# Turning keys and values of heads 1 to 3 in 32x32 blocks on VectorE with transfers, in place of TensorE transposes

## The chip, the cores and the metric

The kernel runs on one core of one Trainium2 chip. The time is the device time of one execution in microseconds (us), as the median of several runs; one execution was also profiled, and all rows below are from that one. PE is TensorE, DVE is VectorE, ACT is ScalarE, POOL is GpSimd, and SP is the engine that issues nearly all transfers (DMAs).

## The reference

The kernel computes one inference step of a decoder layer for a prompt (512 tokens and 16 meta tokens) and 8 samples of 8 tokens, 592 tokens together, in float32. The part that matters here is branch B, a matrix memory with 4 heads of width 256:

```python
z  = xn @ w_in + b_in          # columns split into ... q | k | v | o ...
s  = einsum('bhtd,bhsd->bhts', q, k) * w
num = einsum('bhts,bhsv->bhtv', s, v) + e_int[..., None] * einsum('bhtd,bhdv->bhtv', q, C)
C_new = decay[..., None, None] * C + einsum('bhs,bhsd,bhsv->bhdv', wk, k, v)
```

The projections come out of TensorE with features on the partitions and tokens along the row. The scores need k in that form. The products with `s` and `wk` contract over tokens, so they need k and v the other way round, with tokens on the partitions. That turned form is what the change makes in another way.

## The kernel before

The 592 tokens are padded to 640 = 5 chunks of 128 (`TT` = 5, `TW` = 640). A head is worked off in one turn of the loop `for h in range(HEADS)`, which every engine has in its own program. In the turn of head `h` TensorE does two things in alternation: the attention work of head `h` (`score(c)`, `values(c)` for chunks c = 0 to 4) and the eight projection tiles of head `h + 1`, `fill(h + 1, n)` for n = 0 to 7. Tiles 0 and 1 are the keys, 2 and 3 the values, 4 and 5 the queries, 6 and 7 the output gate (`PARTS`). Each tile is 48 matmuls (split float32) on one 128-column slice of the weights. Tiles 5 to 7 are cut in twelve pieces, `mix(0)` to `mix(11)`, that lie between the steps of `values(4)` (the chunk with the samples). The piece behind `mix(2)` is the product of the queries with the eight sample states; TensorE waits there for all eight state loads, `c_in[0]` to `c_in[7]`.

For heads 1 to 3, keys and values are turned inside the turn of the head before. `k_tokens(h + 1)` runs after tile 2, `v_tokens(h + 1)` after tile 4, and `last_tokens(h + 1)` (the fifth chunk of both) inside `values(4)`: 8 + 8 + 4 TensorE transposes of 128x128 into PSUM (`ring`), which ScalarE copies to `k_tok` (`kt`) and `v_tok` (`vt`). For head 0 the same happens before the loop.

Weights come through two `stage` slots. SP issues the load of a tile's weights when POOL has finished with the slot (`w_lo`); ScalarE then makes the high part `whi` (L924), POOL the low part `wlo` (L866), and TensorE waits for `w_lo`. SP works strictly in the order of its program, so a wait in it holds back everything behind. Its turn of the loop is:

```python
for n in range(2 if h else 3, 8):
    ...
    head_load(8 * (h + 1) + n)     # weights of tile n of head h + 1
c_load(h, 6)                       # states 6 and 7 of this head, into v_feat
c_load(h, 7)                       # both wait until last_tokens(h + 1) is done
next_load(h, 0)
```

States 6 and 7 are loaded into `v_feat` (`vf`), the buffer from which the values are turned; that is why they wait for the turning.

Of the kernel before, what the change touches and what calls it, by code (L numbers as in the profile page):

```python
# [31 lines left out]
P = 128  # L32
# [72 lines left out]
for h_ in range(-1, HEADS):  # L105

    names = [("proj", h_ + 1, n_) for n_ in range(8)]
    if h_ < 0:

        names[7:7] = [("ltok", 0)]  # L110
        names[6:6] = [("ktok", 0)]
    elif h_ + 1 < HEADS:
        names[5:5] = [("vtok", h_ + 1), ("ltok", h_ + 1)]
        names[3:3] = [("ktok", h_ + 1)]
    for name_ in names:
        TILES[name_] = T_NEXT
        T_NEXT += 1
    if h_ < 0:

        T_WA = T_NEXT  # L120
        T_NEXT += 8
# [138 lines left out]
def hybrid_layer(nc, a, o):  # L260
    w_in, b_in = a["w_in"][0], a["b_in"][0]
    ctx = ExitStack()
    with ctx:
# [151 lines left out]
        ones = sb("ones", [P, P], r + 512)  # L415
        wt = [sb("w_t0", [P, TW], r + 1024), wt1]
        gq = sb("gate_rows", [P, TW], r + 1024 + 4 * TW)
        r += 1024 + 8 * TW
        nst = sb("n_state", [P, NS, 8], r)
        misc = sb("misc", [P, 256], r + 288)  # L420
# [56 lines left out]

            return (m0, HALF), (HALF, T)

        def turned(name, h):  # L480

            if h:
                return wide[TILES[name, h] % 2]
            return bank2(1 if name == "ltok" else 0)

        def ffn_out(n):
# [39 lines left out]
        sq_done, var_done, root_done, nt_scaled, ht_done, head_done = (  # L526
            sem("sq_done"), sem("var_done"), sem("root_done"), sem("nt_scaled"), sem("ht_done"), sem("head_done"))
        x_free = sem("x_free")
        n_turned, n_ready = sem("n_turned"), sem("n_ready")
        guard_ready = sem("guard_ready")  # L530
        qz_zero, pad_zero = sem("qz_zero"), sem("pad_zero")
# [16 lines left out]

        def aview(ap):
            return ap.rearrange("(r c) -> r c", c=P)  # L550

        block = ctx.enter_context(nc.Block())

# [2 lines left out]
        def _(sp):  # L556
# [124 lines left out]
            def c_load(h, idx):  # L681

                if h:
                    sp.wait_ge(c_out[idx], 16 * h)
                if h + 1 == HEADS and idx in (4, 5):

                    sp.wait_ge(head_done, 2 * (HEADS - 1))
                if h + 1 < HEADS and idx >= 6:

                    sp.wait_ge(tile_done, TILES["ltok", h + 1] + 1)  # L690
                sp.dma_start(state(h, idx), a["state_mlstm_C"][0, ORDER[idx], h].rearrange("(i p) v -> p i v", p=P)
                             ).then_inc(c_in[idx], 16)

# [34 lines left out]
            def next_load(h, j):  # L728
# [3 lines left out]
                else:  # L732
                    sp.wait_ge(w_lo, B_WB + j - 1)
                    load(B_WB + j, (B_WB + j) % 2, wb, slice(P * j, P * j + P))

            for h in range(HEADS):
                for n in range(2 if h else 3, 8):
                    if h + 1 == HEADS and n in (5, 6):
                        c_load(h, n - 1)
                    head_load(8 * (h + 1) + n)  # L740

                c_load(h, 6)
                c_load(h, 7)
                next_load(h, 0)
                sp.wait_ge(z_evicted, NZ * h + TT)
                sp.dma_start(o["p_mlstm_C"][0, 0, h].rearrange("(i p) v -> p i v", p=P), cp[h % 2][:, :, 0:DH]
                             ).then_inc(cp_out, 16)
                for idx in range(4):
                    c_store(h, idx)
                next_load(h, 1)  # L750
                if h + 1 < HEADS:
                    for idx in range(4):
                        c_load(h + 1, idx)
                for idx in range(4, 8):
                    c_store(h, idx)
                if h + 2 < HEADS:
                    c_load(h + 1, 4)
                    c_load(h + 1, 5)
                    spread_load(h + 2)
# [156 lines left out]
        def _(act):  # L916
# [242 lines left out]
            def k_tokens(h):  # L1159

                t, s = TILES["ktok", h], h % 2
                evict(t, kt[s][:, 0:4].rearrange("p c d -> p (c d)"), turned("ktok", h)[:, 0:4 * DH], ACT.Copy)

            def v_tokens(h):

                s, z = h % 2, turned("ltok", h)
                dst, src = vt[s][:, 0:4, 0:DH], grouped(turned("vtok", h)[:, 0:4 * DH], DH)
                t = TILES["ltok", h]
                if h:
                    evict(TILES["vtok", h], dst, src, ACT.Copy)  # L1170
                    act.wait_ge(tile_done, t + 1)
                else:

                    act.wait_ge(tile_done, t + 1)
                    st(act.activation(dst, src, ACT.Copy))
                st(act.activation(kt[s][:, 4], z[:, 0:DH], ACT.Copy))
                evict(t, vt[s][:, 4, 0:DH], z[:, DH:2 * DH], ACT.Copy)

# [57 lines left out]
            for h in range(HEADS):  # L1236
                for n in range(8):
                    project_hi(8 * (h + 1) + n)
                    if 1 <= n <= TT:
                        squares(h, n - 1)  # L1240
                    if n == 6:
                        norm_root(h)
                    if n == 7 and h + 1 == HEADS:
                        for f in range(6):
                            act.wait_ge(x_free, f // 2 + 1)
                            hb_split(f)
                    project(8 * (h + 1) + n)
                    if h + 1 < HEADS:
                        if n == 2:
                            k_tokens(h + 1)  # L1250
                            spread(h + 1)
                        elif n == 4:
                            v_tokens(h + 1)


            act.wait_ge(tile_done, T_WB)
# [140 lines left out]
        def _(dve):  # L1397
# [312 lines left out]
            def hb_rest(f):  # L1710

                dve.wait_ge(hb_hi, f + 1)
                tt(xl[:, f, M0:], hb[:, f, M0:], xh[:, f, M0:].bitcast(F32), ALU.subtract).then_inc(hb_lo, 1)

            for h in range(HEADS):
                s = h % 2
                ebc, cpr = ebcs[s], cp[s]
# [26 lines left out]
                for c in range(TT):  # L1744
# [33 lines left out]
                        dve.wait_ge(y_done, n + 1)  # L1778
                        cpy(nt[:, c, :], Y(n)).then_inc(y_evicted, 1)  # L1779

                    if c == 0:
                        dve.wait_ge(tile_evicted, TILES["ltok", h] + 1)
                    if c < 4:
                        keys(c, w[:, P - 1:P])
                        y_evict()
                        update_prompt()
                        if c == 1 and h + 1 < HEADS:
                            mask_add(h + 1)
                        continue
                    keys(c, w[:, TAIL - 1:TAIL])  # L1790
                    for p in range(2):
                        at = PAIR + LS * p + LS - 1
                        st.link(dve.tensor_reduce(wsum[:, p:p + 1], w[:, at:P:2 * PAIR], axis=AX.X, op=ALU.add))
                        keys(TT + p, wsum[:, p:p + 1])
# [28 lines left out]
                    if h + 1 == HEADS:  # L1823
                        hb_rest(0)
                        hb_rest(1)
                    for j in range(2):
                        f = 2 * h + j
                        gcol = cols[:, C_HG + f:C_HG + f + 1]
# [174 lines left out]
        def _(pe):  # L2003
# [206 lines left out]

            def k_tokens(h):

                if h:
                    begin(TILES["ktok", h])
                else:
                    pe.wait_ge(lru_sig, 8)
                    pe.wait_ge(tile_evicted, TILES["proj", 0, 1] + 1)
                tokens(turned("ktok", h), k[h % 2], range(4)).then_inc(tile_done, 1)

            def v_tokens(h):  # L2220

                if h:
                    begin(TILES["vtok", h])
                    tokens(turned("vtok", h), vf, range(4)).then_inc(tile_done, 1)
                else:
                    pe.wait_ge(tile_evicted, TILES["ktok", 0] + 1)
                    tokens(turned("vtok", h), vf, range(4))

            def last_tokens(h):

                if h:
                    begin(TILES["ltok", h])
                pe.wait_ge(pad_zero, min(h + 1, 2))
                tokens(turned("ltok", h), k[h % 2], [4])
                tokens(turned("ltok", h), vf, [4], DH).then_inc(tile_done, 1)

            for n in range(8):
                if 16 + n in LRU_TURN:
# [28 lines left out]
            for h in range(HEADS):  # L2267
# [20 lines left out]
                def values(c):  # L2288

                    n, kap = TT * h + c, NZ * h + c  # L2290
                    pe.wait_ge(p_done, n + 1)
                    if n >= 2:
                        pe.wait_ge(y_evicted, n - 1)
                    last = pe.matmul(Y(n), pt[:, :], vt[s][:, c, :], start=True, stop=c == 0, skip_group_check=True)  # L2294
# [28 lines left out]
                        return  # L2323

                    w = wt[s][:, P * c:TW]
                    for ii in range(2):
                        pe.matmul(NU(n)[:, 16 * ii:16 * ii + 16], kt[s][:, c, P * ii:P * ii + P], w[:, LS - 1:P:LS],
                                         start=False, stop=True, skip_group_check=True)
                    if h + 1 < HEADS:
                        last_tokens(h + 1)  # L2330
                    mix(0)
                    across(P * c, LAST, False)
                    outer()
# [57 lines left out]
                for c in range(TT):  # L2391
                    values(c)
                    if c < 4:
                        score(c + 1)
                        fill(h + 1, c + 1)
                    if h + 1 < HEADS:
                        if c == 1:
                            k_tokens(h + 1)
                        elif c == 3:
                            v_tokens(h + 1)  # L2400

            for f in range(2):
                gemm(B_WB + f, T_WB + f, (B_WB + f) % 2, (T_WB + f) % 2, KT, xh, xl,
# [142 lines left out]
```

## Time and profile before

| | us |
|---|---|
| median of 3 runs (1076.96 to 1077.76) | 1077.06 |
| the profiled execution | 1075.73 |
| its span in the profile | 1073.7 |
| TensorE busy (99% of the span) | 1062.7 |
| VectorE busy (57%) | 608.4 |
| ScalarE busy (37%) | 396.2 |
| GpSimd busy (35%) | 371.6 |
| mean granted TensorE clock | 0.998 |

The three turns that turn keys and values each take 72.9 us or so: the second begins its tile 3 behind 347.35 us, the third behind 420.22 us. Times "at 347.35" are from the start of the span. The profiled execution ran 1.3 us below the median, and 2.0 us of it lie outside the span.

### The profile page before, as it was taken

To read this page: it belongs to the slowest core of one execution; us is meant where nothing else is said; L and a number is where in the kernel's file an instruction comes from. 1 tells how busy PE (TensorE), PEld (TensorE's weight loads), DVE (VectorE), ACT (ScalarE), POOL (GpSimd) and SP (SyncE) were. 2 spreads that over 40 slices of the span, in tenths; PEclk is the share of its full clock that TensorE was granted. 3 is DMA by queue.
4 is the path that set the end of the run, shared out by engine and by line. 5 is a ranking of instruction groups with operands and counts; after the bars stand their busy time and mean duration, and the time that the engine had idled before them with its cause. 6 is when DMAs were issued, how large, how long until landed. Compare 5 with 4: busy or idle time off the path is not lost.

```text
span 1073.7 us, 19483 instructions
## 1 busy us (share of the span) xinstructions
PE 1062.7 (99%) x8034; PEld 1037.8 (97%) x8034; DVE 608.4 (57%) x961; ACT 396.2 (37%) x574; POOL 371.6 (35%) x179
## 2 busy tenths in 40 slices
PE   8999999999999999999999999999999999999997
PEld 7999999999999999999999999999999999999997
DVE  6777458944343242253453338999950189999413
ACT  6566786313332434322432343222311122222332
POOL 4333334332222222222223344333443244334330
PEclk9999999999999999999999999999999999999999
DMA  8433332236254261363442333232323222233312
GB/s 224 136 100 91 103 88 69 79 103 162 59 186 123 71 224 54 89 199 89 140 166 80 91 89 97 81 95 81 101 62 99 74 79 79 79 90 100 99 43 89
DMA packets 180272, 111.80 MB, mean 104 GB/s; under 512 B 7611, under 2 KB 176811, under 8 KB 179934
## 3 DMA queue, kind: packets, MB, share of 16 engines
q1 hardware_dynamic: 179980, 110.55, 35.9%
q8 instruction: 63, 1.03, 0.4%
q14 instruction: 19, 0.16, 0.0%
q10 hardware_dynamic: 210, 0.07, 0.0%
HBM read 93.56 MB, written 14.83 MB: 101 GB/s over the span
## 4 chain that ended last, share of the span: by engine, by line
PE 98%; ACT 1%; POOL 0%; issue 0%; DVE 0%; POOLq 0%; DVEq 0%
PE ring L2017 48%; PE ring L2447 22%; PE bank L2447 17%; PE bank L2314 2%; PE bank L2301 1%; PE bank L2064 1%; PE bank L2284 1%; PE bank L2294 1%; PE bank L2356 1%; PE bank L2174 1%; PE bank L2344 1%; PE ring L2207 1%; PE bank L2379 0%; POOL xl L878 0%; PE bank L2038 0%; PE bank L2493 0%
## 5 line engine op out<-in xcount | busy, mean ns | idle before, releaser
L866 POOL TENSOR_TENSOR wlo<-stage,whi 128x1024 fp32r<-128x1024 f32 x78 | 194.6, 2495 | 417.7 <-ACT whi L924 417.7
L2017 PE MATMUL ring<-xh,whi 128*128 128x256 f32 (+1 forms) x1008 | 223.5, 303 | 0.0
L2017 PE MATMUL ring<-xh,wlo 128*128 128x256 f32 (+1 forms) x1008 | 217.5, 298 | 0.0
L2017 PE MATMUL ring<-xl,whi 128*128 128x256 f32 (+1 forms) x1008 | 217.1, 296 | 0.0
L2017 PEld LDWEIGHTS ring<-xh,whi 128*128 128x128 f32 x1008 | 168.5, 189 | 8.7 <-issue 8.2
L2017 PEld LDWEIGHTS ring<-xl,whi 128*128 128x128 f32 x1008 | 169.6, 189 | 0.0
L2017 PEld LDWEIGHTS ring<-xh,wlo 128*128 128x128 f32 x1008 | 169.5, 189 | 0.0
L924 ACT ACTIVATE whi<-stage 128x1024 fp32r<-128x1024 f32 x80 | 84.3, 1053 | 88.9 <-PE ring L2017 81.4
L909 POOL TENSOR_TENSOR wlo<-stage,whi 128x1024 fp32r<-128x1024 f32 x28 | 71.9, 2567 | 108.2 <-ACT whi L1286 108.2
L1402 DVE SCALAR_TENSOR_TENSOR conv<-up,cols,conv 128x592 f32<-128x592 f32 x88 | 75.5, 858 | 3.1
L1924 DVE TENSOR_SCALAR conv<-up,cols 128x592 f32<-128x592 f32 x44 | 71.9, 1633 | 3.4 <-DVE product L1940 0.5
L1779 DVE COPY num_tok<-bank 128x257 f32<-128x257 f32 x20 | 8.5, 426 | 94.6 <-PE bank L2301 76.3
L909 POOL TENSOR_TENSOR wlo_third<-stage,whi_third 128x1024 fp32r<-128x1024 f32 x16 | 40.7, 2544 | 58.7 <-ACT whi_third L1286 58.7
L1322 ACT ACTIVATE conv<-conv 128x592 f32<-128x592 f32 x22 | 15.4, 700 | 116.1 <-DVE conv L1402 116.1
L912 POOL TENSOR_TENSOR wlo<-stage,whi 128x1408 fp32r<-128x1408 f32 x12 | 38.7, 3232 | 52.9 <-ACT whi L1288 52.9
L2447 PE MATMUL ring<-xl,whi 128*128 128x256 f32 (+1 forms) x256 | 54.9, 295 | 0.0
L2447 PE MATMUL ring<-xh,wlo 128*128 128x256 f32 (+1 forms) x256 | 54.8, 296 | 0.0
L2447 PE MATMUL ring<-xh,whi 128*128 128x256 f32 (+1 forms) x256 | 54.5, 294 | 0.0
L1286 ACT ACTIVATE whi<-stage 128x1024 fp32r<-128x1024 f32 x28 | 29.5, 1054 | 63.6 <-PE ring L2447 42.9
L1968 DVE TENSOR_TENSOR resid<-ring,resid 128x576 f32<-128x576 f32 x9 | 6.8, 758 | 69.6 <-PE ring L2447 69.6
L1912 DVE COPY up<-cols 128x16 f32<-128x16 f32 x44 | 44.6, 1014 | 0.0
L2447 PEld LDWEIGHTS ring<-xh,whi 128*128 128x128 f32 x256 | 43.2, 189 | 0.0
(383 smaller groups left out, 2348.1 us busy)
## 6 DMA issues: line engine op xcount, KB each, us to landing
stage<-in_w_in SPq DMA_DIRECT2D x56, 512.0 KB, 4.2
stage<-in_w_up SPq DMA_DIRECT2D x44, 512.0 KB, 3.8
stage<-in_w_down SPq DMA_DIRECT2D x16, 704.0 KB, 4.6
stage<-in_w_branch_a SPq DMA_DIRECT2D x8, 512.0 KB, 3.9
c_sample<-in_state_mlstm_C SPq DMA_DIRECT2D x16, 256.0 KB, 5.6
out_s_mlstm_C<-c_sample SPq DMA_DIRECT2D x16, 256.0 KB, 2.3
stage<-in_w_branch_b SPq DMA_DIRECT2D x8, 512.0 KB, 4.0
stage<-in_w_out SPq DMA_DIRECT2D x8, 512.0 KB, 3.8
```

What stands on the lines that cost most here:

```text
L866: pool.tensor_tensor(spaced(wlo[:, slot]), packed(stage[:, slot, 0:n]), spaced(whi[:, slot]).bitcast(F32), ALU.subtract).then_inc(w_lo, 1)
L909: pool.tensor_tensor(spaced(l_), packed(stage[:, b % 2, 0:D]), spaced(w_).bitcast(F32), ALU.subtract).then_inc(w_lo, 1)
L912: pool.tensor_tensor(l_, stage[:, b % 2, :], w_.bitcast(F32), ALU.subtract).then_inc(w_lo, 1)
L924: act.activation(spaced(whi[:, slot]), packed(stage[:, slot, 0:n]), ACT.Copy).then_inc(w_hi, 1)
L1286: act.activation(spaced(ffn_weight(i)[0]), packed(stage[:, b % 2, 0:D]), ACT.Copy).then_inc(w_hi, 1)
L1322: act.activation(cv[:, 1, 0:CV_N], cv[:, 1, 0:CV_N], ACT.Gelu_apprx_tanh).then_inc(gelu_done, 1)
L1402: return stt(out=out, in0=in0, scalar=scalar, in1=in1, op0=op0, op1=op1)
L1912: st(cpy(grouped(U[:, US0:UW_F - UG], UG)[:, :, 0:FW - 1], hist[:, :, ft:ft + UPT + 1:UPT]))
L1924: st.link(ts(c_, U[:, 0:CV_N], w[0], bias, ALU.mult, ALU.add))
L2017: last = pe.matmul(of(z, t0, t1), w[:, kk * WS:kk * WS + P], x[:, kk, t0:t1], start=kk == 0 and m == 0, stop=kk == kn - 1 and m == 2)
L2314: lz = pe.matmul(ZP[:, ii], kw[kappa % 3][:, P * ii:P * ii + P], vt[s][:, c, :], start=True, stop=True, skip_group_check=True)
L2447: last = pe.matmul(of(z, t0, t1), w_[:, kk * step:kk * step + P], x_[:, kk, t0 - at:t1 - at], start=kk == 0 and m == 0, stop=kk == kn - 1 ...
```

## The change

For heads 1 to 3 the TensorE transposes and the ScalarE copies behind them are gone, and so are their tiles in the PSUM ring. In their place VectorE transposes 128x640 at a time, which turns each 32x32 block in itself (`turn_blocks`, four instructions a head, into two spare buffers, `turn_tmp`), and SP puts the blocks in place with transfers inside SBUF (`spread_blocks`): 16 for each half of the keys and 16 for each half of the values, 64 a head, 192 in all. One such transfer is 32 partitions by 5 runs of 32 elements (128 bytes), 20 KB. Head 0 is turned as before.

```diff
@@ tiles of the PSUM ring
-    elif h_ + 1 < HEADS:
-        names[5:5] = [("vtok", h_ + 1), ("ltok", h_ + 1)]
-        names[3:3] = [("ktok", h_ + 1)]
@@ buffers and semaphores
+        turn_tmp = [gq[:, :], flat(hb[:, 4:6])[:, 0:TW]]
+        kv_turned = sem("kv_turned")
+        kt_in, vt_in = [sem("kt_in0"), sem("kt_in1")], [sem("vt_in0"), sem("vt_in1")]
+        def moved(h):
+
+            return 16 * 32 * ((h + 1) // 2)
@@ SP: c_load
                 if h + 1 < HEADS and idx >= 6:
 
-                    sp.wait_ge(tile_done, TILES["ltok", h + 1] + 1)
+                    sp.wait_ge(kv_turned, 4 * (h + 1))
@@ SP
+            def spread_blocks(h, dst, arrived, turned_):
+
+                for j in range(2):
+                    sp.wait_ge(kv_turned, turned_ + j + 1)
+                    for a_ in range(4):
+                        for b_ in range(4):
+                            sp.dma_start(dst[32 * b_:32 * b_ + 32, :, P * j + 32 * a_:P * j + 32 * a_ + 32],
+                                         turn_tmp[j].rearrange("p (c t) -> p c t", t=P)
+                                         [32 * a_:32 * a_ + 32, :, 32 * b_:32 * b_ + 32]).then_inc(arrived, 16)
+
             for h in range(HEADS):
                 for n in range(2 if h else 3, 8):
                     if h + 1 == HEADS and n in (5, 6):
                         c_load(h, n - 1)
                     head_load(8 * (h + 1) + n)
+                    if n == 6 and h + 1 < HEADS:
+                        spread_blocks(h + 1, kt[(h + 1) % 2], kt_in[(h + 1) % 2], 4 * h)
+                if h + 1 < HEADS:
+                    spread_blocks(h + 1, vt[(h + 1) % 2], vt_in[(h + 1) % 2], 4 * h + 2)
 
                 c_load(h, 6)
                 c_load(h, 7)
@@ ScalarE, in the turn of a head
-                    if h + 1 < HEADS:
-                        if n == 2:
-                            k_tokens(h + 1)
-                            spread(h + 1)
-                        elif n == 4:
-                            v_tokens(h + 1)
+                    if h + 1 < HEADS and n == 2:
+                        spread(h + 1)
@@ VectorE
+            def turn_blocks(h, src, n):
+
+                dve.wait_ge(tile_evicted, TILES["proj", h, n] + 1)
+                if n == 3:
+                    dve.wait_ge(kt_in[h % 2], moved(h))
+                elif h > 1:
+                    dve.wait_ge(vt_in[(h - 1) % 2], moved(h - 1))
+                for j in range(2):
+                    dve.transpose(turn_tmp[j], src[:, j, :]).then_inc(kv_turned, 1)
+
-                    if c == 0:
-                        dve.wait_ge(tile_evicted, TILES["ltok", h] + 1)
+                    if c == 0 and h == 0:
+                        dve.wait_ge(tile_evicted, TILES["ltok", 0] + 1)
+                    elif c == 0:
+                        dve.wait_ge(kt_in[s], moved(h))
...
+                        if c == 2 and h + 1 < HEADS:
+                            turn_blocks(h + 1, k[(h + 1) % 2], 1)
                         continue
                     keys(c, w[:, TAIL - 1:TAIL])
+                    if h + 1 < HEADS:
+                        turn_blocks(h + 1, vf, 3)
@@ TensorE
+                    if h and c == 0:
+                        pe.wait_ge(vt_in[s], moved(h))
...
+                    if h:
+                        pe.wait_ge(kt_in[s], moved(h))
                     for ii in range(2):
                         pe.matmul(NU(n)[:, 16 * ii:16 * ii + 16], kt[s][:, c, P * ii:P * ii + P], w[:, LS - 1:P:LS],
                                          start=False, stop=True, skip_group_check=True)
-                    if h + 1 < HEADS:
-                        last_tokens(h + 1)
...
-                    if h + 1 < HEADS:
-                        if c == 1:
-                            k_tokens(h + 1)
-                        elif c == 3:
-                            v_tokens(h + 1)
```

SP, first turn of the loop (head 0). Before, five weight loads (tiles 3 to 7), then the two state loads into `v_feat`, then the next weight load:

```order
L562 DMA stage<-in_w_in 128x8x128 [waits w_lo] x5
L691 DMA v_feat<-in_state_mlstm_C 128x2x256 [waits tile_done] x2
L562 DMA stage<-in_w_in 128x8x128 [waits w_lo]
L746 DMA out_p_mlstm_C<-c_prompt_102 128x2x256 [waits z_evicted]
L697 DMA out_s_mlstm_C<-c_sample 128x2x256 [waits z_evicted] x4
```

The same place with the change (`gate_rows` and `hb` are the two halves of `turn_tmp`):

```order
L564 DMA stage<-in_w_in 128x8x128 [waits w_lo] x4
L744 DMA k_tok_81<-gate_rows 32x5x32 [waits kv_turned]
L744 DMA k_tok_81<-gate_rows 32x5x32 x15
L744 DMA k_tok_81<-hb 32x5x32 [waits kv_turned]
L744 DMA k_tok_81<-hb 32x5x32 x15
L564 DMA stage<-in_w_in 128x8x128 [waits w_lo]
L744 DMA v_tok_83<-gate_rows 32x5x32 [waits kv_turned]
L744 DMA v_tok_83<-gate_rows 32x5x32 x15
L744 DMA v_tok_83<-hb 32x5x32 [waits kv_turned]
L744 DMA v_tok_83<-hb 32x5x32 x15
L693 DMA v_feat<-in_state_mlstm_C 128x2x256 [waits kv_turned] x2
L564 DMA stage<-in_w_in 128x8x128 [waits w_lo]
```

The state loads now stand behind 64 transfers, and the weight load of tile 7 behind 32 of them.

VectorE, first turn, from the values step of chunk 3 to chunk 4. Before:

```order
L1751 TENSOR_TENSOR p_t<-w_t_140,bank 128x128 [waits y_done,w_done,scores]
L1758 TENSOR_SCALAR k_w_114<-k_tok_80,w_t_140 128x256 [waits z_done]
L1793 TENSOR_REDUCE misc<-w_t_140 128x1
L1758 TENSOR_SCALAR k_w_115<-k_tok_80,misc 128x256 [waits z_done,dve_step]
L1793 TENSOR_REDUCE misc<-w_t_140 128x1
```

The same place with the change:

```order
L1768 TENSOR_TENSOR p_t<-w_t_140,bank 128x128 [waits y_done,w_done,scores]
L1775 TENSOR_SCALAR k_w_114<-k_tok_80,w_t_140 128x256 [waits z_done]
L1730 STREAM_TRANSPOSE gate_rows<-v_feat 128x640 [waits kt_in1,tile_evicted]
L1730 STREAM_TRANSPOSE hb<-v_feat 128x640
L1816 TENSOR_REDUCE misc<-w_t_140 128x1
L1775 TENSOR_SCALAR k_w_115<-k_tok_80,misc 128x256 [waits z_done,dve_step]
L1816 TENSOR_REDUCE misc<-w_t_140 128x1
```

The turning of the values has come in, with a wait for all 32 transfers of the keys (`kt_in1`), since they read the same two buffers.

## Rows read from the trace of the kernel before

**Rows 1.** The page: span, engines, and the chain that ended last.

```profile
span 1073.7 us, 19483 instructions
PE 1062.7 (99%) x8034; PEld 1037.8 (97%) x8034; DVE 608.4 (57%) x961; ACT 396.2 (37%) x574; POOL 371.6 (35%) x179
...
PE 98%; ACT 1%; POOL 0%; issue 0%; DVE 0%; POOLq 0%; DVEq 0%
```

**Rows 2.** Timeline of PE: start us, us, instruction, count.

```profile
347.35 1.04 PE L2207 MATMUL ring<-ident,k 128*128 128x128 f32 x8
348.23 0.60 PE L2294 MATMUL bank<-v_tok,p_t 128*128 128x257 f32 x2
...
366.42 1.04 PE L2207 MATMUL ring<-ident,v_feat 128*128 128x128 f32 x8
367.29 0.60 PE L2294 MATMUL bank<-v_tok,p_t 128*128 128x257 f32 x2
...
368.09 0.42 PE L2207 MATMUL ring<-ident,k 128*128 128x128 f32 x2
...
368.72 0.51 PE L2017 MATMUL ring<-xh,whi 128*128 128x256 f32 x2
...
375.75 1.07 PE L2344 MATMUL bank<-c_sample,q_padded 128*32 128x256 f32 x16
```

**Rows 3.** Timeline of SP in the same turn: start us, us, transfer, count.

```profile
356.73 5.89 SPq L562 DMA_DIRECT2D stage<-in_w_in  x2
...
368.80 0.89 SPq L691 DMA_DIRECT2D v_feat<-in_state_mlstm_C  x2
```

**Rows 4.** Timeline of ACT in the same turn.

```profile
348.75 1.02 ACT L940 ACTIVATE k_tok<-ring 128x1024 f32<-128x1024 f32 x1
...
353.16 1.04 ACT L924 ACTIVATE whi<-stage 128x1024 fp32r<-128x1024 f32 x1
```

**Rows 5.** DVE: timeline of the same turn, then a group of lines (us, mean ns).

```profile
350.60 0.75 DVE L1402 SCALAR_TENSOR_TENSOR c_prompt<-c_prompt,e_int,bank 128x514 f32<-128x514 f32 x1 [0.44 <-PE bank L2314]
...
L1545 DVE TENSOR_TENSOR lru_r<-u 128x616 f32<-128x616 f32 x8 | 6.4, 799 | 28.3 <-ACT u L1073 28.3
```

**Rows 6.** Timeline of SP: trains of transfers issued back to back.

```profile
10.66 0.70 SPq L606 DMA_DIRECT2D lru_w_r<-in_lru_w_r  x1
...
20.37 0.99 SPq L562 DMA_DIRECT2D stage<-in_w_in  x1
...
51.85 0.60 SPq L654 DMA_DIRECT2D uc_swapped<-uc  x1
...
1023.60 0.36 SPq L803 DMA_DIRECT2D out_s_ffn_conv<-f_out  x1
...
1027.83 0.32 SPq L803 DMA_DIRECT2D out_s_ffn_conv<-f_out  x1
```

**Rows 7.** DMA issues: count, KB each, median us from issue to landing.

```profile
stage<-in_w_in SPq DMA_DIRECT2D x56, 512.0 KB, 4.2
...
uc_swapped<-uc SPq DMA_DIRECT2D x14, 154.0 KB, 4.5
v_feat<-in_state_mlstm_C SPq DMA_DIRECT2D x8, 256.0 KB, 3.4
...
x_tok<-in_meta_tokens SPq DMA_DIRECT2D x1, 64.0 KB, 2.2
```

**Rows 8.** DMA queues: packets, MB, share of 16 engines.

```profile
q1 hardware_dynamic: 179980, 110.55, 35.9%
```

**Rows 9.** Stretches at the end (us, PE busy, granted clock, DMA), then PE's first transposes.

```profile
1068.00:1070.00 2.00, 0.00 (x0) 1.00 1.03 414
1070.00:1072.00 2.00, 0.00 (x0) 0.58 0.99 326
...
3.03 2.39 PE L2038 MATMUL bank<-ident 128*128 128x128 f32 x10
...
12.33 1.25 PE L2038 MATMUL bank<-ident 128*128 128x128 f32 x10
```

More of the change, by code:

```diff
@@ L478, in halves, with turned @@
             return (m0, HALF), (HALF, T)
-        def turned(name, h):
-            if h:
-                return wide[TILES[name, h] % 2]
+        def turned(name):
             return bank2(1 if name == "ltok" else 0)
@@ L1161, in k_tokens @@
                 t, s = TILES["ktok", h], h % 2
-                evict(t, kt[s][:, 0:4].rearrange("p c d -> p (c d)"), turned("ktok", h)[:, 0:4 * DH], ACT.Copy)
+                evict(t, kt[s][:, 0:4].rearrange("p c d -> p (c d)"), turned("ktok")[:, 0:4 * DH], ACT.Copy)
             def v_tokens(h):
-                s, z = h % 2, turned("ltok", h)
-                dst, src = vt[s][:, 0:4, 0:DH], grouped(turned("vtok", h)[:, 0:4 * DH], DH)
+                s, z = h % 2, turned("ltok")
+                dst, src = vt[s][:, 0:4, 0:DH], grouped(turned("vtok")[:, 0:4 * DH], DH)
                 t = TILES["ltok", h]
[L1169 to L1175, printed above, removed]
+                act.wait_ge(tile_done, t + 1)
+                st(act.activation(dst, src, ACT.Copy))
                 st(act.activation(kt[s][:, 4], z[:, 0:DH], ACT.Copy))
@@ L1825, in _ @@
                         hb_rest(1)
+                    elif h + 2 == HEADS:
+                        dve.wait_ge(vt_in[(h + 1) % 2], moved(h + 1))
                     for j in range(2):
@@ L2211, in k_tokens @@
             def k_tokens(h):
[L2213 to L2218, printed above, removed]
-            def v_tokens(h):
[L2222 to L2227, printed above, removed]
-            def last_tokens(h):
[L2231 to L2235, printed above, removed]
+                pe.wait_ge(lru_sig, 8)
+                pe.wait_ge(tile_evicted, TILES["proj", 0, 1] + 1)
+                tokens(turned("ktok"), k[h % 2], range(4)).then_inc(tile_done, 1)
+            def v_tokens(h):
+                pe.wait_ge(tile_evicted, TILES["ktok", 0] + 1)
+                tokens(turned("vtok"), vf, range(4))
+            def last_tokens(h):
+                pe.wait_ge(pad_zero, 1)
+                tokens(turned("ltok"), k[h % 2], [4])
+                tokens(turned("ltok"), vf, [4], DH).then_inc(tile_done, 1)
             for n in range(8):
```

## The prediction

> **What bounds the kernel now.** I read the page first. TensorE is busy for 1062.7 of the 1073.7 us, and the chain that ended last is 98% PE [rows 1]. So what leaves PE's program is gained in full, and what makes PE wait is lost in full. The other engines matter only through what PE waits for. Next I read PE's timeline in the second of the three turns that change. Take the end of projection tile 2, 347.35, as local zero. Keys are turned from 347.35 to 348.23, values from 366.42 to 367.29, the last chunk from 368.09 to 368.72, and PE reaches the product with the sample states at 375.75, local 28.4 [rows 2]. There it waits for all eight state loads. SP's timeline then says when those arrive: the weight load of tile 6 is issued at 356.73 (the first of the two in that row), and the last two state loads leave at 368.80 [rows 3] and land 3.4 us behind their issue [rows 7], at about 372.7. PE gets there 3 us later and doesn't wait. That is the whole cover these loads have.
>
> **What is removed.** On PE 20 transposes a head. From start to start the first eight cost 0.88 us, the next eight 0.87 and the last four 0.63 [rows 2], together 2.38 us a head and 7.1 us for three heads. Nothing on PE takes their place. ScalarE loses its copies; the one of the keys takes 1.02 us and stands before the high part of the weights of tile 4, which began at 353.16 [rows 4]. That part comes 1.02 us earlier, and so does what hangs on it. ScalarE's own gain is worth nothing, since PE is the path.
>
> The page "VectorE: DVE Perf Modes" of the Trainium skill (Rules for kernel authors) speaks against this change: a 128x128 transpose belongs on TensorE if its result may lie in PSUM. It prices one at 390 ns in bf16 (The three transpose paths). By that figure the removal would be an estimated 23 us. The trace disagrees, since the transposes follow each other every 0.11 us [rows 2], and I go by the trace.
>
> **What is added on VectorE.** Four transposes of 128x640. The trace has none. The nearest row is an elementwise pass over 128x616 at 799 ns [rows 5], so I take 0.8 us; they can't be free, and twice that would add only 0.8 us to the chain below, where one of them stands. Those of the keys start when the update of chunk 2 ends, at 350.60 + 0.75 [rows 5], and are done before SP is ready for them.
>
> **What is added on SP.** 64 transfers a head, issued one behind the other. This decides. Their price is not in the trace, and the rows around it are wide apart. The cheapest train has 13 small stores from 1023.60 to 1027.83, which is 0.35 us from start to start. A mixed train has 17 loads of parameters from 10.66 to 20.37, or 0.57 each. The only transfers from SBUF to SBUF, 64 partitions each, hold SP 0.60 us [rows 6]. The new ones are also SBUF to SBUF, but with 32 partitions, between the 16 of the cheapest train and those 64. I take R = 0.50 us each, with 0.35 and 0.70 as ends.
>
> **The chain in one turn,** in local time with the saved PE time taken out:
> - Tile 6's load is issued at 9.4 before, less 1.02, so 8.4. SP is free of it at 8.8 (0.44 us a transfer, half of the 0.89 for two in [rows 3]).
> - The 32 transfers of the keys: 32 R = 16.0, until 24.8. Tile 7's weights leave then, at 25.2, and land by 29.4 (4.2 us, [rows 7]). They can wait: tile 7's first matmuls are behind the point where PE is going to stand.
> - VectorE may overwrite the buffers only when the keys have landed. The last transfer leaves at 24.3; landing takes 2.2 us for a small load and 4.5 for the SBUF copies [rows 7]; I take 3.0, so 27.3. Then one transpose, 28.1.
> - The 32 transfers of the values, until 44.1.
> - The two state loads; the second leaves at 44.6 and lands 3.4 us later, at 48.0.
> - PE is there at 28.4 - 2.4 = 26.0, and stands for 22.0 us.
>
> Written with R this is 64 R - 10.0 us a head, three times: 66.0 us. VectorE stands meanwhile from its keys step of chunk 4 until 27.3, with the sample weights of the keys, the update of the prompt state and the eviction of chunk 4 behind it. PE asks for those only behind the product for which it waits, so this is covered by the longer stall. If R were so small that there is no stall, it would cost nothing either. The turned keys and values themselves are wanted only in the next turn, more than 30 us of PE work later, and are covered. When PE goes on, SP is again waiting for PE, so the delay is not carried further, and it occurs once in each of the three turns.
>
> **The clock.** At the end of the run PE has nothing to do from 1068 at the latest; the granted clock is 1.00 until 1070 and 0.58 in the two us behind, so it falls to its lower level (1.2 GHz of 2.4) within some 4 us [rows 9]. A stall of 22 us must do the same. How long the low level then lasts is not seen behind a stall. At the start, PE's first ten transposes take 2.39 us, ten like them at 12.33 take 1.25 [rows 9], so there the slow pace lasts at least 2.4 us. I take twice that, 5 us at half pace, a loss of 2.5 us a turn and 7.5 in all; ends 0 and 10.
>
> **The sum.** 1075.7 (the profiled run) - 7.1 + 66.0 + 7.5 = 1142.1. The median of the runs is 1.3 us above the profiled one, so 1143.4; I say 1143. VectorE's four instructions and the wait in its queue are in it with the 0.8 us of the chain.
>
> **The rivals.**
> *Cheap issue.* SP issues the new transfers like the small stores, R = 0.35. For it: they have few partitions and move 20 KB each. Against it: they have 160 runs on both sides, and both sides lie in SBUF. Then 12.4 us a head, and 1077.1 - 7.1 + 37.2 + 7.5 = 1114.7.
> *The transfer engines are the limit.* 32 transfers are 5120 runs of 128 bytes, 320 for each of 16 engines. All packets of the run took 35.9% of 16 x 1073.7 us for 179980 [rows 1, 8], 34 ns each and on average 614 bytes; at that pace 320 take 11 us, less than SP's 16. It decides from 50 ns a packet on. At 100 ns one transfer costs 1.0 us, the stall is 54 us, and the time 1077.1 - 7.1 + 162 + 7.5 = 1239.5. The page "DMA: Bandwidth & Descriptors" of the Trainium skill says both things: below 512 bytes there is read-modify-write (Specifications), but small pieces are slow only with HBM, not between SBUF and SBUF (Why small descriptors are slow). By the first this rival gains, by the second it falls away; no row of before has a packet of 128 bytes between SBUF and SBUF.
> *The transfers are hidden, and the kernel is faster.* The place is again the wait for the state loads. 64 R - 10.0 falls below the 2.38 us saved at R = 0.193. 512 KB of weights land in 4.2 us [rows 7]; if the 640 KB of one tensor cost only their bytes, 5.3 us or R = 0.16, PE would stand 0.5 us, and the time would be 1077.1 - 7.1 + 1.5 = 1071.5. Against it: no train in the rows is below 0.35 us. The same page (Issuing engines are not separate DMA queues) calls the time to initiate a DMA usually small relative to the DMA; that rule is this rival. The SBUF copies hold SP 0.60 us and land after 4.5 [rows 6, 7], which agrees for one of them, but with 32 in a row the issue adds up and the landing overlaps.
> *No change* would need R near 0.19 too, with the same row against it.
>
> **Chances.** Forecast, R from 0.42 to 0.72: 0.55. Cheap issue, R below 0.42 but with a stall: 0.28. Transfer engines or a still dearer issue: 0.13. Hidden and faster: 0.02; within 0.2% of before (which is about what a measurement of this kernel can tell from no change): 0.02. The forecast's own range is from R = 0.42 (16.9 us a head) to 0.72 (36.1), 1128 to 1186. The range for 8 in 10 takes in most of the cheap case, from R = 0.33 (11.1 us a head, 1111) down by the open clock term to 1106, and ends at 1186. Faster 0.02, same 0.02, slower 0.96.
>
> **What the changed profile would show.** PE idle three times, each time ahead of the product with the states (the line of L2344 before), for about 22 us, put down to a DMA of `v_feat`. SP busy in two blocks of 32 transfers a turn, of 16 us each, with a gap of some 4 us between them, in which VectorE waits for `kt_in`. Granted clock at half behind each stall. Tiles 3 and 4 unchanged in pace, no wait for weights. The chain of work should then show SP and DMA. It would be wrong if the gap lay elsewhere (PE waiting for `w_lo`, for VectorE's evictions or for `vt_in`), if one transfer took less than 0.35 us of SP, or if the landing of the last block took far longer than 3 us, which would mean that the engines and not SP set the pace.

## The result: 1077.0 to 1166.4 us, and the profile after

The changed kernel takes 1166.38 us (median of 4 runs, 1165.78 to 1168.7) against 1077.01 for the kernel before in the same series; the ratio is 1.0839, interval 1.0825 to 1.0852. It is slower by 89 us. The forecast was 1143 with a range of 1106 to 1186.

The page of the profile after, as in [rows 1], and PE's longest waits (us in total, times, longest us):

```profile
span 1164.6 us, 19549 instructions
...
PE 1060.3 (91%) x7974; PEld 1033.0 (89%) x7974; DVE 619.9 (53%) x973; ACT 388.0 (33%) x562; POOL 371.5 (32%) x179
...
PEclk9999999999779959976999999999999999999999
...
q1 hardware_dynamic: 213772, 114.49, 35.2%
```

```profile
PE bank L2362 <- DMA v_feat<-in_state_mlstm_C: 92.5, 3, 31.7
PE ring L2058 <- POOL misc L861: 2.8, 1, 2.8
```

PE's busy time hardly changed, 1062.7 before and 1060.3 after; some of the work behind each stall ran at the slow clock, which hides part of what was removed (the same work without a stall takes 1055.4, below). What is new is one wait, three times, 30.8 us on average, at the product with the sample states, for a transfer into `v_feat`. The clock line has three dips at the same places. 33792 packets have come in, 176 for each of 192 transfers.

SP in the second turn, which answers to [rows 3] (start us, us, transfer, count), and VectorE's entry in the same turn:

```profile
384.71 0.37 SPq L564 DMA_DIRECT2D stage<-in_w_in  x1
385.13 10.61 SPq L744 DMA_DIRECT2D k_tok<-gate_rows  x16
395.78 10.98 SPq L744 DMA_DIRECT2D k_tok<-hb  x16
406.80 0.59 SPq L564 DMA_DIRECT2D stage<-in_w_in  x1
408.96 10.32 SPq L744 DMA_DIRECT2D v_tok<-gate_rows  x16
419.33 10.33 SPq L744 DMA_DIRECT2D v_tok<-hb  x16
429.76 1.05 SPq L693 DMA_DIRECT2D v_feat<-in_state_mlstm_C  x2
```

```profile
408.08 0.85 DVE L1730 STREAM_TRANSPOSE gate_rows<-v_feat 128x640 f32<-128x640 f32 x1 [17.53 <-DMA k_tok<-hb]
```

And PE at the end of the same stall, to be held against [rows 2]:

```profile
401.98 0.50 PE L2355 MATMUL bank<-ones,q_n 128*128 128x1 f32 x4
433.52 1.93 PE L2362 MATMUL bank<-c_sample,q_padded 128*32 128x256 f32 x16 [31.04 <-DMA v_feat<-in_state_mlstm_C]
```

Read from the top: SP issues transfers without a break from 385.13 to 429.66, except for 1.6 us in which VectorE waits for the last keys to land and turns the first values. Only then do the two state loads leave. PE has asked for them since 402.5. Sixteen transfers take 10.3 to 11.0 us, so one is 0.65 to 0.69 us from start to start. Before, the state loads of [rows 3] left 7 us before PE needed them.

### The profile page after: what moved, and what is told of

The parts are those of the page before. It is cut to its first block, busy times and chain, and to the rows that moved or that the text cites. A ratio compares the mean times of both kernels' runs of the same rounds, so it can differ in the third digit from the quotient of the medians.

```text
span 1164.6 us, 19549 instructions
## 1 busy us (share of the span) xinstructions
PE 1060.3 (91%) x7974; PEld 1033.0 (89%) x7974; DVE 619.9 (53%) x973; ACT 388.0 (33%) x562; POOL 371.5 (32%) x179
## 4 chain that ended last, share of the span: by engine, by line
PE 54%; issue 34%; POOL 6%; SPq 3%; ACT 1%; DMA 0%; DVE 0%; POOLq 0%; DVEq 0%
PE ring L2460 21%; PE bank L2460 15%; PE ring L2042 15%; POOL wlo L882 6%; SPq L744 3%; PE bank L2362 0%; PE bank L2332 0%; PE bank L2374 0%; POOL xl L894 0%; PE bank L2319 0%; DMA v_feat<-in_state_mlstm_C 0%; PE bank L2063 0%; PE bank L2506 0%; ACT x_raw L992 0%; ACT xh L1004 0%
## 5 line engine op out<-in xcount | busy, mean ns | idle before, releaser
L2042 PEld LDWEIGHTS ring<-xh,whi 128*128 128x128 f32 x1008 | 169.1, 190 | 9.0 <-issue 8.5
L2362 PE MATMUL bank<-c_sample,q_padded 128*32 128x256 f32 x64 | 6.9, 570 | 92.5 <-DMA v_feat<-in_state_mlstm_C 92.5
L2362 PEld LDWEIGHTS bank<-c_sample,q_padded 128*32 128x32 f32 x64 | 2.5, 146 | 94.1 <-issue 93.9
L1236 ACT ACTIVATE num_sq<-num_tok 128x256 f32<-128x256 f32 x20 | 8.2, 408 | 132.4 <-DVE num_tok L1796 132.4
```

Source lines behind the costliest of these rows:

```text
L2042: last = pe.matmul(of(z, t0, t1), w[:, kk * WS:kk * WS + P], x[:, kk, t0:t1], start=kk == 0 and m == 0, stop=kk == kn - 1 and m == 2)
L2362: last = pe.matmul(Y(n)[32 * j:32 * j + 32, 0:DH], qz[:, ii, ORDER[4 * g + j], :], state(h, 4 * g + j)[:, ii, :], start=False, stop=g == 1 ...
```

## The experiments

Three theories. A: SP needs a fixed time for each transfer, whatever is in it, and the state loads stand in its queue behind 64 of them. B: the transfer engines set the pace, by 128-byte packets. C: the cost is VectorE's wait for the landed keys, before it may reuse its buffers. The code cuts show only the lines that carry the change; `...` marks what lies between.

### The price of a transfer by itself

Behind the end of the kernel before, trains of one shape each, with a wait for landing between them. The first of nine:

```diff
+            for i in range(16):
+                p0, x0 = 32 * (i % 4), 32 * (i // 4)
+                sp.dma_start(d5[p0:p0 + 32, :, x0:x0 + 32], v5[x0:x0 + 32, :, p0:p0 + 32]).then_inc(probe, 16)
+            n_ += 16
+            landed()
```

> The kernel before, with copies behind its end that nobody needs, in trains of one shape each; only SP's time for one and the landing are read, the total time grows by some 100 us and says nothing. Theory A (SP pays a price per transfer, whatever is in it): 32 partitions x 5 runs of 128 bytes from SBUF to SBUF cost 0.65 us from start to start as in the changed kernel, and so do 32 x 1 run and 32 x 640 contiguous bytes; fewer partitions (16) perhaps 0.35. Theory B (the transfer engines set the pace through the number of 128-byte packets): 32 x 1 run falls to 0.35 or so, 64 x 5 runs rises to 1.3, 128 x 5 runs to 2.6.

SP's timeline. In order: copies inside SBUF of 32 partitions x 5 runs of 128 bytes, 32 x 1 run, 32 x 640 bytes in one piece, 16 x 5 runs, 64 x 5 runs, 128 x 5 runs, 128 x 2560 bytes; then stores of 32 x 20 runs of 128 bytes and loads of 32 x 5 runs of 512 bytes.

```profile
1076.99 10.41 SPq L845 DMA_DIRECT2D probe_dst<-probe_src  x16
1088.65 10.30 SPq L850 DMA_DIRECT2D probe_dst<-probe_src  x16
1100.08 10.01 SPq L855 DMA_DIRECT2D probe_dst<-probe_src  x16
1111.28 10.24 SPq L860 DMA_DIRECT2D probe_dst<-probe_src  x16
1122.74 10.65 SPq L865 DMA_DIRECT2D probe_dst<-probe_src  x16
1134.83 5.47 SPq L869 DMA_DIRECT2D probe_dst<-probe_src  x8
1142.55 2.44 SPq L873 DMA_DIRECT2D probe_dst<-probe_src  x4
1147.51 10.96 SPq L878 DMA_DIRECT2D probe_dram<-probe_src  x16
1160.16 10.24 SPq L884 DMA_DIRECT2D probe_dst<-probe_dram  x16
```

0.61 to 0.69 us each, from 16 to 128 partitions and from 4 KB to 320 KB. Where theory B wanted 1.3 and 2.6 us for 64 and 128 partitions, the rows say 0.67 and 0.68. Theory A was wrong in one guess: 16 partitions are no cheaper.

### Why the cheapest train was cheap, and two issuers

More trains in the same manner, and the 32 x 5 copies from SP and ACT at once.

```diff
+            for i in range(12):
+                m = 2 if i % 2 else 16
+                sp.dma_start(qdram[i, 0:m], src[16 * (i % 8):16 * (i % 8) + m, 0:1024].rearrange("p (g x) -> p g x", x=P)
+                             ).then_inc(probe, 16)
...
+                act.dma_start(da[p0:p0 + 32, :, x0:x0 + 32], va[x0:x0 + 32, :, p0:p0 + 32]).then_inc(probe_a, 16)
```

> The kernel before with more trains behind its end (its total time says nothing): stores of 16 x 8 rows and 2 x 8 rows in turn as in the kernel's own cheap train, stores of 16 x 8 rows alone, stores of 32 rows, stores of 8 rows, copies of 8 rows inside SBUF, and last the 32 x 5 copies from SP and from ACT at once. Theory A in the form that every transfer on 16 engines costs 0.65 us and one on 8 or fewer 0.35: the first train alternates or averages near 0.35, 16 x 8 and 32 rows cost 0.65, 8 rows 0.35 in both directions. For the two issuers: if the price is each engine's own, 0.65 in both; if they share one generator of descriptors, 1.3 in both.

SP's timeline: stores of 16 x 8 and 2 x 8 rows in turn, of 16 x 8 rows, of 32 rows, of 8 rows; copies of 8 rows inside SBUF; the last train beside ACT's, whose row stands below it.

```profile
1077.49 4.00 SPq L848 DMA_DIRECT2D probe_q<-probe_src  x12
1082.74 5.60 SPq L853 DMA_DIRECT2D probe_q<-probe_src  x12
1090.15 5.41 SPq L858 DMA_DIRECT2D probe_r<-probe_src  x12
1096.62 3.98 SPq L862 DMA_DIRECT2D probe_s<-probe_src  x12
1101.55 8.11 SPq L866 DMA_DIRECT2D probe_dst<-probe_src  x12
1110.77 10.44 SPq L871 DMA_DIRECT2D probe_dst<-probe_src  x16
```

```profile
1110.77 10.79 ACTq L1443 DMA_DIRECT2D probe_act<-probe_src  x16
```

Stores into one solid piece outside SBUF cost 0.33 to 0.47 us; the same 8 rows copied inside SBUF cost 0.68. So the cheap train of [rows 6] was cheap for its destination; few partitions and a small size are not enough, though among the stores 8 rows (0.33) are cheaper than 32 (0.45). The form "16 engines dear, 8 engines cheap" is refuted twice: 8-row copies cost 0.68, and stores of 16 x 8 and of 32 rows 0.47 and 0.45 where it wanted 0.65. Why the train that alternates 16 x 8 with 2 x 8 rows stays at 0.33 on average, below the 0.47 of 16 x 8 alone, is open. SP and ACT side by side each keep 0.65 to 0.67, so the price belongs to each issuing engine.

### Four fifths of the bytes left out

This kernel leaves out the moving of four of the five chunks: they hold ones, written once by VectorE, or what head 0 left.

```diff
-                            sp.dma_start(dst[32 * b_:32 * b_ + 32, :, P * j + 32 * a_:P * j + 32 * a_ + 32],
+                            sp.dma_start(dst[32 * b_:32 * b_ + 32, 0:1, P * j + 32 * a_:P * j + 32 * a_ + 32],
...
-                                         [32 * a_:32 * a_ + 32, :, 32 * b_:32 * b_ + 32]).then_inc(arrived, 16)
+                                         [32 * a_:32 * a_ + 32, 0:1, 32 * b_:32 * b_ + 32]).then_inc(arrived, 16)
```

> The changed kernel with its 192 transfers at their places, but each moves only the first of its 5 runs (4 KB instead of 20 KB); the other chunks of the turned keys and values are filled with ones or left from head 0, so the work left out is four fifths of the bytes moved. Theory A (SP's time per transfer): nothing changes, 0.65 us each, 1166 us within 3. Theory B (128-byte packets in the transfer engines): a fifth of the packets, 0.35 us each, a stall of 12 us instead of 31 a turn, about 1112 us.

1164.25 us, ratio 1.0818 (1.0796 to 1.0840). 24576 packets fewer than in the changed kernel, and only 2 us of the 89 are gone; PE's wait for the states is 89.3 us in all against 92.5. Theory B falls for this kernel.

### Half of the transfers left out

This kernel leaves out every second transfer; VectorE writes ones, once, where head 1's blocks would have gone.

```diff
-            return 16 * 32 * ((h + 1) // 2)
+            return 16 * 16 * ((h + 1) // 2)
...
-                        for b_ in range(4):
+                        for b_ in range(0, 4, 2):
```

> The changed kernel at its own order with every second transfer left out (96 instead of 192, 32 a head); the partitions that are not filled are ones or left from head 0, so half of the blocks are not moved. Theory A (stall = 64 R - 10.0 us a turn with R = 0.65, here 32 R - 10.0): 10.8 us a turn instead of the measured 30.8, and since the weight load ahead of tile 0 of the next head is not pushed behind anything new, no wait for weights: 1166.4 - 60 = 1106 us within 5. Rival (a stall once there brings other waits of its own, as with the state loads first at 1128): a wait for the low part of the weights comes back, 1120 us or more.

1107.20 us, ratio 1.0275 (1.0258 to 1.0292). PE's longest waits; the second is the one at the start of the run:

```profile
PE bank L2367 <- DMA v_feat<-in_state_mlstm_C: 32.4, 3, 12.1
PE ring L2063 <- POOL misc L861: 2.8, 1, 2.8
```

That is 10.8 us a turn, as expected, and no wait for weights. Cutting the number by 32 a turn takes 20.0 us off the stall, 0.63 each; cutting four fifths of the content took off 1.1. This and the run before are the clearest pair.

### The state loads ahead of the values' transfers

```diff
-                if h + 1 < HEADS:
-                    spread_blocks(h + 1, vt[(h + 1) % 2], vt_in[(h + 1) % 2], 4 * h + 2)
-
                 c_load(h, 6)
                 c_load(h, 7)
+                if h + 1 < HEADS:
+                    spread_blocks(h + 1, vt[(h + 1) % 2], vt_in[(h + 1) % 2], 4 * h + 2)
+
                 next_load(h, 0)
```

> The two state loads are issued ahead of the 32 transfers of the values, nothing else. Theory A (the state loads are late because SP is still issuing what stands before them): 32 x 0.65 = 20.7 us less a turn, a stall of 10 us instead of 31, 1166 - 62 = 1104 us. Theory C (VectorE's wait for the landed keys before it may reuse its buffers is the costly one): that wait stays 17 us a turn, and the time stays above 1140 us.

1127.96 us, ratio 1.0476 (1.0458 to 1.0493). PE's waits, and VectorE's wait for the keys in this kernel:

```profile
PE bank L2362 <- DMA v_feat<-in_state_mlstm_C: 31.3, 3, 11.5
PE ring L2042 <- POOL wlo L882: 14.6, 4, 5.2
```

```profile
DVE gate_rows L1730 <- DMA k_tok<-hb: 51.5, 3, 18.0
```

The stall for the states is 10.4 us a turn, as A said. VectorE's wait is as long as in the changed kernel (51.7 us in all there), yet 61 us of stall are gone, so C falls: that wait is almost wholly the 32 transfers of the keys, and PE feels it only through the state loads. The time missed A's 1104 by 24 us. The next head's first weight load stands behind the values' transfers, as it did in the changed kernel, but PE no longer stands still meanwhile, and it waits 14.6 us for weights. The rest is the clock, which this placement makes slow more often: 1128.0 - 1068.4 (the time without transfers, below) - 31.3 - 14.6 leaves 13.7, and PE is busy 14.0 us longer with the same instructions (1069.4 against the 1055.4 without transfers).

### The next weight load ahead of them too

```diff
-                if h + 1 < HEADS:
-                    spread_blocks(h + 1, vt[(h + 1) % 2], vt_in[(h + 1) % 2], 4 * h + 2)
-
                 c_load(h, 6)
                 c_load(h, 7)
                 next_load(h, 0)
+                if h + 1 < HEADS:
+                    spread_blocks(h + 1, vt[(h + 1) % 2], vt_in[(h + 1) % 2], 4 * h + 2)
```

> As with the state loads first, but the next head's first weight load also stands ahead of the values' transfers. Theory A: the waits for the low part of the weights (14.6 us in four places, behind them a slow clock) shrink to the next weight load alone, which comes 20 us late behind the same transfers; the stall for the states stays at 10 us a turn; 1128 falls to 1105-1112 us. Rival: the lateness is only handed on to the stores and loads behind and the time stays at 1125 us or more.

1122.74 us, ratio 1.0433 (1.0412 to 1.0453). The expected range was missed; the rival came near. PE waits 30.2 us for the states and still 11.9 for weights, in five places. SP in the second turn, from the values' transfers on:

```profile
397.11 0.46 SPq L564 DMA_DIRECT2D stage<-in_w_in  x1
397.62 10.71 SPq L744 DMA_DIRECT2D v_tok<-gate_rows  x16
408.38 11.48 SPq L744 DMA_DIRECT2D v_tok<-hb  x16
...
422.88 0.72 SPq L564 DMA_DIRECT2D stage<-in_w_in  x1
...
435.15 28.23 SPq L564 DMA_DIRECT2D stage<-in_w_in  x5
```

The load of tile 0 is early now, but those of tile 1 (422.88) and tile 2 (435.15) come late behind the 22 us block and what piled up behind it. PE stands for both, at 431.7 and 446.2. With some 42 us of issue for the blocks in a turn that takes 71 us without stalls, moving one load out of the way hands the lateness to the next.

### No transfers at all

The moving of the blocks is left out: `spread_blocks` and the waits for it are gone, and VectorE fills `k_tok` and `v_tok` of heads 1 and 3 once with ones:

```diff
-                    if n == 6 and h + 1 < HEADS:
-                        spread_blocks(h + 1, kt[(h + 1) % 2], kt_in[(h + 1) % 2], 4 * h)
-                if h + 1 < HEADS:
-                    spread_blocks(h + 1, vt[(h + 1) % 2], vt_in[(h + 1) % 2], 4 * h + 2)
...
-                if n == 3:
-                    dve.wait_ge(kt_in[h % 2], moved(h))
-                elif h > 1:
-                    dve.wait_ge(vt_in[(h - 1) % 2], moved(h - 1))
+                if h == 1:
+                    dst = kt[1][:, :] if n == 1 else vt[1][:, :, 0:DH]
+                    dve.memset(dst, 1.0).then_inc(kt_in[1] if n == 1 else vt_in[1], 1)
```

> The changed kernel without its 192 transfers and the waits for them: VectorE still turns the blocks, TensorE and ScalarE do not; the turned keys and values of heads 1 and 3 are ones, those of head 2 are head 0's, so moving the blocks is left out. Theory A: only TensorE's saving is left, 1077.0 - 7.1 = 1069.9 us within 1. Rival: VectorE's four transposes a head cost something on the path, or the saving was mostly hidden; then 1073 to 1077 us.

1068.43 us against 1076.19, ratio 0.9928 (0.9911 to 0.9944). Its page:

```profile
PE 1055.4 (99%) x7974; PEld 1030.5 (97%) x7974; DVE 620.5 (58%) x975; ACT 387.9 (36%) x562; POOL 370.9 (35%) x179
```

So the half of the change that takes turning off TensorE is worth 7.8 us, and VectorE's part costs nothing that shows. With PE's program as it is, a way of moving the blocks that PE never waits for ends here. The instructions on PE are as many as in the changed kernel (7974), which is busy 4.9 us longer with them; that is the loss by the clock there.

### Through memory outside SBUF, with 32 transfers a head

In the change one copy inside SBUF moves one block column. Written out by groups of 32 partitions, with its 128-byte pieces at their final place, and read back in pieces of 512 bytes, half as many transfers do. VectorE's buffers are free when the stores have landed, and the state loads and the next weight load come first:

```diff
+                    for a_ in range(4):
+                        sp.dma_start(tdram[h, m, j][:, :, 32 * a_:32 * a_ + 32],
+                                     turn_tmp[j][32 * a_:32 * a_ + 32].rearrange("p (g x) -> p g x", x=32)
+                                     ).then_inc(t_out[j], 16)
...
+                    for b_ in range(4):
+                        sp.dma_start(dst[32 * b_:32 * b_ + 32, :, P * j:P * j + P], tdram[h, m, j][:, b_:20:4, :]
+                                     ).then_inc(arrived, 16)
...
+                        store_blocks(h + 1, 0)
...
                 c_load(h, 6)
                 c_load(h, 7)
+                if h + 1 < HEADS:
+                    store_blocks(h + 1, 1)
                 next_load(h, 0)
+                if h + 1 < HEADS:
+                    place_blocks(h + 1, 0, kt[(h + 1) % 2], kt_in[(h + 1) % 2])
+                    place_blocks(h + 1, 1, vt[(h + 1) % 2], vt_in[(h + 1) % 2])
```

> The blocks go through memory outside SBUF: 4 stores and 4 loads for each half instead of 16 copies, 32 a head instead of 64, VectorE may reuse its buffers as soon as the 8 stores of the keys have landed, and the state loads and the next weight load stand ahead of all loads back. Theory A (SP's time at about 0.65 us per transfer, and its order): the state loads leave about 19 us behind the end of tile 2 and land at 22, PE asks at 26, so no stall and 1069 us, the time without transfers (1068.4) within 1.5. Rival: the pieces of 128 bytes are slow in that memory, or 32 transfers still push a load past its time; then a stall of 2 to 5 us a turn and 1076 to 1090 us.

1068.34 us (1068.15 to 1069.67) against 1075.86, ratio 0.9930 (0.9916 to 0.9943). It beats both kernels, the one before by 0.7%. SP in the second turn:

```profile
353.80 3.27 SPq L745 DMA_DIRECT2D blocks_turned<-gate_rows  x4
357.12 2.69 SPq L745 DMA_DIRECT2D blocks_turned<-hb  x4
359.85 0.63 SPq L566 DMA_DIRECT2D stage<-in_w_in  x1
362.39 0.89 SPq L695 DMA_DIRECT2D v_feat<-in_state_mlstm_C  x2
...
370.05 5.15 SPq L754 DMA_DIRECT2D k_tok<-blocks_turned  x8
375.24 5.14 SPq L754 DMA_DIRECT2D v_tok<-blocks_turned  x8
```

The state loads leave at 362.4, 2.6 us after SP is done with the first 8 stores, and PE waits for nothing in the loop; its longest wait in the whole run is the 2.8 us at the start. The price of one transfer is much the same: 0.64 us for the loads back, 0.67 to 0.82 for the stores. The number and the places are different, and this run does not say which of the two does how much.

## Why the prediction was right, and which term was off

**The bound and the place.** Right. PE was the path, and the only wait of any size that came in on PE is the one named, at the product with the states, in each of the three turns. One sign did not come as said: the chain of work of the changed kernel's page is PE 54%, issue 34%, SP's queue 3% and DMA 0%, so it hardly shows the transfers; the waits do.

**The removal.** 7.1 us from [rows 2]; measured with the rest taken away, 7.8. The trace was right against the estimate of 23 us: "VectorE: DVE Perf Modes" of the Trainium skill (The three transpose paths) prices a transpose on TensorE at 390 ns in bf16, and here 20 of them a head, in float32, were worth 2.6 us, 0.13 each.

**VectorE.** Predicted 0.8 us for a transpose of 128x640, measured 0.80 to 0.85.

**SP.** This is the mis-sized term. I took R = 0.50 us, between the cheapest train and the copies of `uc_swapped` in [rows 6]; it is 0.65, and 0.61 to 0.68 for every copy inside SBUF that I tried. The nearest row in kind (SBUF to SBUF, 0.60) had it nearly right, and counting partitions to interpolate was the mistake. At 0.15 us too little, 64 transfers in three turns make 28.8 us. That the time stayed in the range is owed to its width, R up to 0.72, and not to the 0.50.

**The formula.** 64 R - 10.0 gives 31.6 us at 0.65; measured 30.8 on average (29.8, 31.0 and 31.7). With half the transfers it gives 10.8; measured 10.8 on average (9.7 in the second turn, 12.1 at most). The last landing of the keys was 1.9 us where I took 3.0, which takes 1.1 off a turn; in the turn shown the transfers cost 0.66 on average, which gives 0.6 of it back and leaves 31.1 against the 31.0 measured there.

**The clock.** A stretch view of the changed kernel (us, PE busy, granted clock, DMA share, GB/s), at the start and the end of the second stall:

```profile
404.00:406.00 2.00, 0.00 (x0) 0.92 0.19 31
406.00:408.00 2.00, 0.00 (x0) 0.50 0.19 31
434.00:435.00 1.00, 1.00 (x16) 0.50 0.90 271
435.00:436.00 1.00, 1.00 (x15) 0.50 0.74 239
436.00:437.00 1.00, 1.00 (x13) 0.79 0.29 99
437.00:438.00 1.00, 1.00 (x9) 1.00 0.00 0
```

PE stopped at 402.5, the clock was at its lower level (1.2 GHz) before 406, and it was back 3 us after PE went on at 433.5. I had 5 us at half pace, a loss of 2.5 a turn. By PE's busy time the loss is 1060.3 - 1055.4 = 4.9, or 1.6 a turn; what is left of the time after the other terms, 1166.4 - 1068.4 - 92.5 = 5.5, agrees.

The row from which I took the length of the slow stretch does not bear it, though. In the kernel before, the view of the clock within the first ten transposes of [rows 9] reads:

```profile
3.00:4.00 1.00, 1.00 (x6) 1.00 1.04 380
```

The granted clock is 1.00 there, so these transposes are not shown to be slow by the clock; what made them slow is open. That the 5 us lay no further from the 3 us measured is luck.

**The sum with measured terms.** 1143.4, plus 28.8 for R, less 3.3 for the landing, 2.6 for the clock and 0.7 for the removal, is 1165.6; measured 1166.4.

**The rivals.** Cheap issue (1115) and transfer engines (1240) did not happen, and the bytes-only case (1071.5) neither. Two statements of "DMA: Bandwidth & Descriptors" of the Trainium skill bear on the rivals. The one that small pieces are slow only with HBM (Why small descriptors are slow) agrees with the copies of 20 KB: 1.9 us to landing with 128-byte runs, 1.8 with 640-byte ones. The other, that the time to initiate a DMA is usually small relative to the DMA (Issuing engines are not separate DMA queues), fits one copy loosely (0.6 against 1.9 us) and misleads for 64 in a row, where the landings overlap and the issues add up.

The reordered kernels show what I had missed in general: I called the delay not carried further. That is true of the change as made, because SP is waiting for PE again behind each stall, and it stopped being true as soon as the state loads were moved ahead.

## What to carry to other kernels

Count transfers before bytes: on a queue that also feeds the engine that bounds the kernel, each one here cost 0.65 us of that queue, and everything behind it is late by the sum. Look for the transfer with the least slack behind the new ones, and price the new ones by a row with the same two memories at its ends. Here the new issues filled more than half of the queue's turn, and both orders that I tried only picked another victim (1128 and 1123 us); half as many transfers in another order, by a detour through another memory, was the cure. Sharing the transfers between SP and ACT was not tried in the kernel.

## What the runs showed that I had not expected

The time that SP needs for a copy inside SBUF is nearly the same for 8 rows of 512 bytes (0.68 us), 32 runs of 128 bytes (0.64) and 128 x 2560 bytes (0.61), while stores of 8 or 32 whole rows to memory outside SBUF cost 0.33 and 0.45. Broken up into runs of 128 bytes, such a store costs 0.69. SP and ACT, both issuing, do not slow each other (0.65 and 0.67 us).
